# A hybrid attention and convolution backbone on one core: where the second stage's input tiles are split into high and low parts

## The chip, the cores and the metric

The kernel runs on one core of one Trainium2 chip. The metric is device microseconds (us) of one execution. Before the change the median of three runs is 3134.49 us (3130.92, 3134.49 and 3137.77).

## What is computed

Two layers over 2048 latent tokens of width 1024, with a context prefix of 256 tokens. Layer 0 is a multi-head latent attention. Layer 1 is a Conformer convolution module, and the change lies at its start:

```python
def conformer_conv_branch(h, w_in, w_dw, b_dw, g_ln, b_ln, w_o):
    a, bgl, g = jnp.split(h @ w_in, 3, axis=-1)
    u = a * jax.nn.sigmoid(bgl)
    u = lax.conv_general_dilated(u, w_dw, window_strides=(1,), padding=[(CONV_PAD, CONV_PAD)],
                                 dimension_numbers=('NWC', 'WIO', 'NWC'),
                                 feature_group_count=CONV_W) + b_dw
    u = jax.nn.silu(layer_norm(u, g_ln, b_ln)) * jax.nn.silu(g)
    return u @ w_o
```

Here `h` is 2048 x 1024 and `w_in` is 1024 x 3072. Everything is float32. A product is made of three TensorE passes over operands that are each split into a rounded high part and a low remainder (high x high, high x low, low x high: `split3`, L93 to L97).

## The kernel before

The program runs five stages one after the other: `front`, `attention`, `attn_out`, `conv_in`, `conv_out`. The change is in `conv_in` (L1444 to L1868), which makes `h @ w_in`, the gates and the depthwise convolution.

**The input.** `h` comes from `attn_out` through memory as 32 tiles of 128 x 512 (256 KB each; tile n is the slice n % 8 of the width and the block n // 8 of the tokens). Each tile passes three steps. SyncE loads it (`load_h`, L1519) into one of four staging buffers: two are the halves of `ci_gb`, two are made of `ci_raw`. ScalarE copies it to the high part (`h_high`, L1602, tile `h1hi`). VectorE subtracts to get the low part (`h_low`, L1780, tile `h1lo`), which frees the buffer: SyncE waits for `h_low` of tile n - 4 before it loads tile n. The high and low parts of all 32 tiles stay in SBUF for the whole stage.

**The groups.** The width of the output is done in 8 groups of 128 channels. In a group TensorE makes for each block b of 512 tokens a product B (the sigmoid's input, bank 2b) and a product A (bank 2b + 1), of 24 matmuls each, and afterwards four gate products G. From the second group on it also does, after each of the eight A and B products, one chunk of the convolution of the group before. Banks are used in turn, n % 6 for the n-th product of a group: the seventh product (B of block 3, here called B3; the names B0, A0, B1, ... follow) goes into the bank of B0 and waits until ScalarE has made the sigmoid of B0 (`s_sig`); the eighth waits until VectorE has multiplied A0 by that sigmoid (`s_mul`). In the first group each B product also waits, slice by slice, for the `h_low` of its own tiles (`s_hlo`): B0 for tiles 0 to 7, B1 for 8 to 15, B2 for 16 to 23, B3 for 24 to 31.

**The order on the engines.** Every engine has a fixed order of its own. Before the change ScalarE and VectorE go through all 32 tiles first, and only then enter the loop over groups (`loop`, `body`), where the first sigmoid, the copy of the third weight (`w_high` of G) and the first product by a sigmoid (`product`, L1702, which makes `ci_ub`) stand. SyncE likewise loads all 32 tiles, waits for the last `h_low`, and only then starts on the taps, the next group's weights (`load_w`, 512 KB each, L1504) and the stores of `ci_ub` (`store_u`, L1536, 256 KB each, written in pieces of 64 numbers). GpSimd has only the bands of the convolution (L1863).

Of the kernel before, what the change touches and what calls it, by code (L numbers as in the profile page):

```python
# [16 lines left out]

# [1 line left out]

# [1422 lines left out]
def conv_in(nc, net, hhi, hlo, z0, zs, qs):  # L1444
# [9 lines left out]
    with nc.cleanup_on_exit(), ExitStack() as st:  # L1454
# [24 lines left out]
        staged = [t[:, r].rearrange("p s n -> p (s n)") for t in (gb,) for r in range(2)] + [  # L1479
            raw[:, 2 * r:2 * r + 2].rearrange("p s n -> p (s n)") for r in range(2)]  # L1480
        NH = NBLK * KD
        block = st.enter_context(nc.Block())
        B, A, G = range(3)

        def h_tile(t, n):
            return t[:, n % KD, n // KD * BLK:(n // KD + 1) * BLK]
# [29 lines left out]
        @block.sync  # L1516
        def _(sp):
            def load_h(n):
                sp.dma_start(staged[n % 4], net.h1[n % KD, :, n // KD * BLK:(n // KD + 1) * BLK]).then_inc(s_h[n % 4], 16)  # L1519

            load_w(sp, 0, B)
            for n in range(4):
                load_h(n)
            load_w(sp, 0, A)
            sp.dma_start(mask[:], net.mask_in).then_inc(s_const, 16)
            sp.dma_start(bdw[:], net.b_dw).then_inc(s_const, 16)
            for n in range(4, NH):
                sp.wait_ge(s_hlo, n - 3)
                load_h(n)
                if n == KD:  # L1530
                    load_w(sp, 0, G)
            sp.wait_ge(s_hlo, NH)

            def store_u(g, b):
                sp.wait_ge(s_mul, g * 8 + (b + 1))
                sp.dma_start(columns(net.u_phases, g, b), ub[:, b % 2]).then_inc(s_ust[b % 2], 16)  # L1536

            def store_gate(g, b):
                sp.wait_ge(s_mul, g * 8 + (NBLK + b + 1))
                sp.dma_start(columns(net.gate1, g, b), gb[:, b % 2]).then_inc(s_gst[b % 2], 16)  # L1540

            def reload_u(g, q):
                if q + 4 < CH:
                    sp.wait_ge(s_ulo, g * CH + (q + 1))
                    load_u(sp, g, q + 4)

            def store_z(g, q):
                sp.wait_ge(s_z, g * CH + (q + 1))
                sp.dma_start(net.z_chunks[bass.ds(g * CH + q, 1)].rearrange("a p n -> p (a n)"),
                             zb[:, q % 2]).then_inc(s_zst[q % 2], 16)  # L1550

            def body(g, first, last):
                if not first:
                    sp.wait_ge(s_tlo, g)
                sp.dma_start(taps[:], net.taps[bass.ds(g, 1)].rearrange("a p q t -> p (a q) t")).then_inc(s_taps, 16)
                for n in range(CH):
                    if not first:
                        reload_u(g - 1, n)
                        if n:
                            store_z(g - 1, n - 1)  # L1560
                    if not last and n < 3:
                        sp.wait_ge(s_wlo, g * 3 + (n + 1))
                        load_w(sp, g + 1, n)
                    if n % 2:
                        store_u(g, n // 2)
                if not first:
                    store_z(g - 1, CH - 1)
                for k in range(2):
                    sp.wait_ge(s_ust[k], g * 32 + 32)
                for q in range(4):  # L1570
                    load_u(sp, g, q)
                if not last:
                    for b in range(NBLK):
                        store_gate(g, b)
                else:
                    for x in TAIL:
                        if isinstance(x, int):
                            reload_u(g, x)
                            store_z(g, x)
                        else:  # L1580
                            store_gate(g, int(x[1]))

            loop(sp, body)
            for k in range(2):
                sp.wait_ge(s_gst[k], 32 * GROUPS)
                sp.wait_ge(s_zst[k], 64 * GROUPS)
# [12 lines left out]
        def _(act):  # L1599
# [5 lines left out]
            for n in range(4):  # L1605
                h_high(n)
            w_high(act, 0, A, True)
            for n in range(4, NH):
                h_high(n)

            def sigmoid(g, n, src, first):
# [30 lines left out]
            def body(g, first, last):  # L1642
                if first:
                    act.wait_ge(s_const, 32)
                    act.wait_ge(s_pad, 1)
                else:
                    u_high(g - 1, 0)
                for n in range(CH):
                    if not first:
                        if n:  # L1650
                            evict_z(g - 1, n - 1)
                        if n + 1 < CH:
                            u_high(g - 1, n + 1)
                    if n % 2 == 0:
                        act.wait_ge(s_ab, g * 8 + (n + 1))
                        sigmoid(g, n // 2, ps[:, n % 6], first)
                    if n == 0:
                        w_high(act, g, G, first)
                if not first:
                    evict_z(g - 1, CH - 1)  # L1660
                if not last:
                    for s in (B, A):
                        w_high(act, g + 1, s, False)
                act.wait_ge(s_taps, g * 16 + 16)
                if not first:
                    act.wait_ge(s_bhi, g * CH)
                nc.scalar.activation(thi[:], taps[:], ACT.Copy).then_inc(s_thi, 1)
                if not last:
                    for b in range(NBLK):
                        gate(g, b)  # L1670
                else:
                    gate(g, 0)
                    u_high(g, 0)
                    u_high(g, 1)
                    for x in TAIL[1:]:
                        if isinstance(x, int):
                            evict_z(g, x)
                            if x + 2 < CH:
                                u_high(g, x + 2)
                        else:  # L1680
                            gate(g, int(x[1]))
# [5 lines left out]
        def _(dve):  # L1687
# [45 lines left out]
            def gate(g, b):  # L1733
                product(g, NBLK + b, gb[:, b % 2], ps[:, (8 + b) % 6],
                        None if isinstance(g, int) and g == 0 and b < 2 else (s_gst[b % 2], g * 32 + 16 * (b // 2)))

            def body(g, first, last):
                if first:
                    dve.wait_ge(s_const, 32)
                else:  # L1740
                    band_and_low(g - 1, 0)
                for n in range(CH):
                    if not first and n + 1 < CH:
                        band_and_low(g - 1, n + 1)
                    if not first and n:
                        chunk_sums(g - 1, n - 1)
                    b = n // 2
                    if n % 2:
                        dve.wait_ge(s_ab, g * 8 + (n + 1))
                        product(g, b, ub[:, b % 2], ps[:, n % 6],  # L1750
                                None if first and b < 2 else (s_ust[b % 2], g * 32 + 16 * (b // 2)))
                    if n == 1:
                        w_low(g, G)
                if not first:
                    chunk_sums(g - 1, CH - 1)
                if not last:
                    for s in (B, A):
                        w_low(g + 1, s)
                dve.wait_ge(s_thi, g + 1)
                if not first:  # L1760
                    dve.wait_ge(s_blo, g * CH)
                nc.vector.tensor_tensor(tlo[:], taps[:], thi[:].bitcast(F32), ALU.subtract).then_inc(s_tlo, 1)  # L1762
                if not last:
                    for b in range(NBLK):
                        gate(g, b)
                else:
                    gate(g, 0)
                    band_and_low(g, 0)
                    band_and_low(g, 1)
                    for x in TAIL[1:]:  # L1770
                        if isinstance(x, int):
                            if x + 2 < CH:
                                band_and_low(g, x + 2)
                            chunk_sums(g, x)
                        else:
                            gate(g, int(x[1]))

            def h_low(n):
                dve.wait_ge(s_hhi, n + 1)
                nc.vector.tensor_tensor(h_tile(hlo, n), staged[n % 4], h_tile(hhi, n).bitcast(F32),  # L1780
                                        ALU.subtract).then_inc(s_hlo, 1)

            w_low(0, B)
            for n in range(4):
                h_low(n)
            w_low(0, A)
            for n in range(4, NH):
                h_low(n)
            loop(dve, body)
            add_squares(GROUPS * CH - 1)  # L1790
# [470 lines left out]
```

## Time and profile before

| what | value |
|---|---|
| median of three runs | 3134.49 us |
| the profiled execution's own time | 3137.61 us |
| its span, first to last instruction | 3135.7 us |
| TensorE busy | 2933.1 us, 94% |
| VectorE busy | 1817.4 us, 58% |
| ScalarE busy | 1448.3 us, 46% |
| GpSimd busy | 430.2 us, 14% |
| mean granted TensorE clock | 0.983 |

`conv_in` runs from about 2251 us to about 2907 us of the span, and its first group of products from 2258 to 2337 us. Busy shares are averages over the whole span; the change touches some 45 us of it, so that it is read from the timeline of that stretch. In a timeline the columns are start (us from the start of the span), duration (us), engine, line, operation, output and inputs, shape, how many were merged, and in brackets how long the engine sat idle before and what ended that.

### The profile page before, as it was taken

To read this page: it belongs to the slowest core of one execution; us is meant where nothing else is said; L and a number is where in the kernel's file an instruction comes from. 1 tells how busy PE (TensorE), PEld (TensorE's weight loads), DVE (VectorE), ACT (ScalarE), POOL (GpSimd) and SP (SyncE) were. 2 spreads that over 40 slices of the span, in tenths; PEclk is the share of its full clock that TensorE was granted. 3 is DMA by queue.
4 is the path that set the end of the run, shared out by engine and by line. 5 is a ranking of instruction groups with operands and counts; after the bars stand their busy time and mean duration, and the time that the engine had idled before them with its cause. 6 is when DMAs were issued, how large, how long until landed. Compare 5 with 4: busy or idle time off the path is not lost. (4 is left out here: it accounts for less than half of the span.)

```text
span 3135.7 us, 44436 instructions
## 1 busy us (share of the span) xinstructions
PE 2933.1 (94%) x14789; PEld 2436.3 (78%) x14789; DVE 1817.4 (58%) x3135; ACT 1448.3 (46%) x3063; POOL 430.2 (14%) x493
## 2 busy tenths in 40 slices
PE   2999999789999999999999999799799999999698
PEld 2877878578887888878787888678578888888587
DVE  6645545366766776767676676544344444445775
ACT  2544545346555565555555565444432222222553
POOL 1000000012222122222122222100001111112000
PEclk9999999899999999999999999899899999999899
DMA  6556454521211111111212110154442222222563
GB/s 218 173 167 214 165 199 153 192 78 41 70 33 47 56 57 57 51 45 39 72 41 69 34 31 28 69 190 161 147 139 76 76 75 70 73 69 63 180 196 123
DMA packets 225010, 316.59 MB, mean 101 GB/s; under 512 B 81920, under 2 KB 143632, under 8 KB 223632
## 3 DMA queue, kind: packets, MB, share of 16 engines
q1 hardware_dynamic: 220176, 305.37, 30.2%
q10 hardware_dynamic: 4608, 8.39, 0.7%
q8 instruction: 119, 1.95, 0.3%
q14 instruction: 107, 0.88, 0.1%
HBM read 213.95 MB, written 99.75 MB: 100 GB/s over the span
## 5 line engine op out<-in xcount | busy, mean ns | idle before, releaser
L1095 DVE TENSOR_TENSOR at_ptlo<-at_T,at_pthi 128x512 fp32r<-128x512 f32 x576 | 396.8, 689 | 325.0 <-ACT at_pthi L972 321.8
L956 ACT ACTIVATE at_prob<-at_S,at_nmax 128x512 f32<-128x512 f32 (+1 forms) x640 | 411.0, 658 | 371.9 <-DVE at_nmax L1070 360.6
L972 ACT ACTIVATE at_pthi<-at_T 128x512 fp32r<-128x512 f32 x576 | 348.7, 608 | 214.1 <-PE at_T L841 214.1
L1059 DVE TENSOR_REDUCE at_mx<-at_S 128x1 f32<-128x512 f32 (+1 forms) x640 | 393.7, 631 | 75.3 <-PE at_S L816 70.7
L841 PE MATMUL at_T<-ident,at_prob 128*128 128x128 f32 x2304 | 345.7, 272 | 3.2 <-DVE at_ptlo L1095 3.2
L841 PEld LDWEIGHTS at_T<-ident,at_prob 128*128 128x128 f32 x2304 | 279.0, 140 | 68.0 <-DVE at_ptlo L1095 12.5
L95 PE MATMUL ci_ps<-h1hi,ci_whi 128*128 128x512 f32 x768 | 301.8, 393 | 18.0 <-DVE h1lo L1780 12.3
L96 PE MATMUL ci_ps<-h1lo,ci_whi 128*128 128x512 f32 x768 | 300.9, 392 | 0.0
L97 PE MATMUL ci_ps<-h1hi,ci_wlo 128*128 128x512 f32 x768 | 300.6, 391 | 0.0
L811 PE MATMUL at_S<-at_khi,at_qhi 128*128 128x512 f32 (+1 forms) x640 | 249.6, 390 | 46.6 <-ACT at_prob L956 23.8
L95 PE MATMUL at_O<-at_pthi,at_vhi 128*128 128x512 f32 x576 | 270.5, 470 | 3.3 <-issue 2.7
L516 DVE TENSOR_TENSOR fr_wlo<-fr_w,fr_whi 128x1024 fp32r<-128x1024 f32 (+1 forms) x99 | 114.6, 1159 | 251.9 <-ACT fr_whi L388 251.7
L815 PE MATMUL at_S<-at_krhi,at_qr 128*128 128x512 f32 (+1 forms) x640 | 239.0, 373 | 0.0
L813 PE MATMUL at_S<-at_khi,at_qlo 128*128 128x512 f32 (+1 forms) x640 | 238.4, 372 | 0.0
L816 PE MATMUL at_S<-at_krlo,at_qr 128*128 128x512 f32 (+1 forms) x640 | 237.8, 372 | 0.0
L812 PE MATMUL at_S<-at_klo,at_qhi 128*128 128x512 f32 (+1 forms) x640 | 237.5, 371 | 0.0
L97 PE MATMUL at_O<-at_pthi,at_vlo 128*128 128x512 f32 x576 | 227.5, 395 | 0.0
L96 PE MATMUL at_O<-at_ptlo,at_vhi 128*128 128x512 f32 x576 | 227.5, 395 | 0.0
L1863 POOL TENSOR_TENSOR ci_blo<-ci_tlo,ci_mask 128x640 fp32r<-128x640 f32 x64 | 108.4, 1701 | 787.2 <-DVE ci_tlo L1762 433.1
L1210 POOL TENSOR_TENSOR at_dgx<-ident,at_rl 128x128 f32<-128x128 f32 x128 | 51.1, 400 | 1079.0 <-DVE at_dghi L1087 1079.0
L95 PE MATMUL fr_ps<-fr_hhi,fr_whi 128*128 128x512 f32 (+1 forms) x472 | 185.3, 393 | 4.9 <-DVE fr_rob L571 1.8
L811 PEld LDWEIGHTS at_S<-at_khi,at_qhi 128*128 128x128 f32 x640 | 120.8, 189 | 83.8 <-ACT at_prob L956 33.2
(221 smaller groups left out, 6116.0 us busy)
## 6 DMA issues: line engine op xcount, KB each, us to landing
fr_w<-in_w_front SPq DMA_DIRECT2D x75, 512.0 KB, 4.1
at_wmod<-in_w_mod SPq DMA_DIRECT2D x32, 512.0 KB, 3.4
ci_w<-in_cv_w_in SPq DMA_DIRECT2D x24, 512.0 KB, 4.1
fr_w<-in_w_front SPq DMA_DIRECT2D x24, 384.0 KB, 4.0
values<-fr_ob SPq DMA_DIRECT2D x36, 256.0 KB, 2.8
at_kst<-k_nope SPq DMA_DIRECT2D x8, 1152.0 KB, 7.6
at_vst<-values SPq DMA_DIRECT2D x8, 1152.0 KB, 8.2
fr_x<-in_x SPq DMA_DIRECT2D x16, 512.0 KB, 6.7
```

The costliest lines, as they stand in the source:

```text
L95: nc.tensor.matmul(out, whi, xhi, start=first, stop=False)
L96: nc.tensor.matmul(out, whi, xlo, start=False, stop=False)
L97: return nc.tensor.matmul(out, wlo, xhi, start=False, stop=last)
L811: nc.tensor.matmul(out, qhi[:, r, q], khi[:, k], start=True, stop=False)
L813: nc.tensor.matmul(out, qlo[:, r, q], khi[:, k], start=False, stop=False)
L815: nc.tensor.matmul(out, qr[:, r, q], krhi[:, k], start=False, stop=False)
L816: nc.tensor.matmul(out, qr[:, r, q], krlo[:, k], start=False, stop=True).then_inc(s_qk, 1)
L841: mm = nc.tensor.transpose(out[:, i * P:(i + 1) * P], prob[:, j % 2, i, kt * P:(kt + 1) * P], net.ident[:])
L956: nc.scalar.activation(prob[:, j % 2, i, k], S[:, c, 0:k.stop - k.start], ACT.Exp, scale=SCALE, bias=nmax[:, i % 2:i % 2 + 1], accum_out=l ...
L972: nc.scalar.activation(dst, T[:, (n + SLOTS * j) % 2], ACT.Copy).then_inc(s_hi, 1)
L1059: nc.vector.tensor_reduce(mx[:, i % 2, c:c + 1], S[:, c, 0:k.stop - k.start], AXX, ALU.max).then_inc(s_mx, 1)
L1095: nc.vector.tensor_tensor(ptlo[:, kt % 3], T[:, (n + SLOTS * j) % 2], pthi[:, kt % 3].bitcast(F32), ALU.subtract).then_inc(s_lo, 1)
```

## The change

In the first group the 32 tiles are no longer all split ahead of the loop. Tiles 0 to 7 are split ahead of it as before. Tiles 8 to 31 are split inside the first body, between its steps n = 0 to 7:

- n = 0: ScalarE does `h_high` of 8 to 11, the first sigmoid, `h_high` of 12 to 15, the weight copy `w_high` of G; VectorE does `h_low` of 8 to 15.
- n = 1: tiles 16 to 19; then VectorE does the first product (`ci_ub`) and `w_low` of G.
- n = 2: tiles 20 to 23, then on ScalarE the second sigmoid.
- n = 3: tiles 24 to 27; then VectorE does the second product.
- n = 4: tiles 28 to 31, then on ScalarE the third sigmoid.

SyncE loads tiles up to 11 ahead of the body, then G's weight (before, that stood behind tile 8) and the taps. Inside the body it loads 12 to 15 and the next group's weight B, 16 to 19 and weight A and `store_u` of block 0, 20 to 23 and weight G, 24 to 27 and `store_u` of block 1, 28 to 31. The wait for the last `h_low` moves behind the stores. TensorE's program and GpSimd's are the same.

```diff
+        def split_behind(n):
+
+            m = KD + 4 * (n + 1)
+            return (range(KD, KD + 4), range(KD + 4, m + 4)) if n == 0 else (range(m, min(m + 4, NH)), range(0))
+
...
-            for n in range(4, NH):
+            def reload_h(n):
                 sp.wait_ge(s_hlo, n - 3)
                 load_h(n)
-                if n == KD:
-                    load_w(sp, 0, G)
-            sp.wait_ge(s_hlo, NH)
+
+            for n in range(4, KD + 4):
+                reload_h(n)
+            load_w(sp, 0, G)
...
                 for n in range(CH):
-                    if not first:
+                    if first:
+                        for x in range(KD + 4 * (n + 1), min(KD + 4 * (n + 2), NH)):
+                            reload_h(x)
+                    else:
                         reload_u(g - 1, n)
                         if n:
                             store_z(g - 1, n - 1)
...
                 for k in range(2):
                     sp.wait_ge(s_ust[k], g * 32 + 32)
+                if first:
+                    sp.wait_ge(s_hlo, NH)
                 for q in range(4):
                     load_u(sp, g, q)
...
             w_high(act, 0, A, True)
-            for n in range(4, NH):
+            for n in range(4, KD):
                 h_high(n)
...
                 for n in range(CH):
-                    if not first:
+                    if first:
+                        for x in split_behind(n)[0]:
+                            h_high(x)
+                    else:
                         if n:
                             evict_z(g - 1, n - 1)
                         if n + 1 < CH:
...
                         act.wait_ge(s_ab, g * 8 + (n + 1))
                         sigmoid(g, n // 2, ps[:, n % 6], first)
+                    if first:
+                        for x in split_behind(n)[1]:
+                            h_high(x)
                     if n == 0:
                         w_high(act, g, G, first)
...
                     if not first and n:
                         chunk_sums(g - 1, n - 1)
+                    if first:
+                        for x in itertools.chain(*split_behind(n)):
+                            h_low(x)
                     b = n // 2
...
             w_low(0, A)
-            for n in range(4, NH):
+            for n in range(4, KD):
                 h_low(n)
             loop(dve, body)
```

## Rows read from the trace of the kernel before

**Rows 1.** The page's first part: busy time, share, instructions of each engine.
```profile
PE 2933.1 (94%) x14789; PEld 2436.3 (78%) x14789; DVE 1817.4 (58%) x3135; ACT 1448.3 (46%) x3063; POOL 430.2 (14%) x493
```
**Rows 2.** Waits of TensorE, 2250 to 2345 us: total us, times, longest us.
```profile
PE ci_ps L95 <- DVE h1lo L1780: 12.3, 2, 10.9
PE ci_ps L95 <- ACT ci_sig L1615: 5.7, 1, 5.7
```
**Rows 3.** Waits of TensorE, 2345 to 2920 us, those in this stage.
```profile
PE ci_ps L95 <- DVE ci_ulo L1730: 0.6, 1, 0.6
```
**Rows 4.** Timeline of TensorE around its wait, start, us, operation.
```profile
2295.12 0.39 PE L97 MATMUL ci_ps<-h1hi,ci_wlo 128*128 128x512 f32 x1
2301.19 0.80 PE L95 MATMUL ci_ps<-h1hi,ci_whi 128*128 128x512 f32 x1 [5.69 <-ACT ci_sig L1615]
...
2306.48 0.41 PE L95 MATMUL ci_ps<-h1hi,ci_whi 128*128 128x512 f32 x1
```
**Rows 5.** Windows: stretch and its us, busy (count) by engine, PEclk, DMA share, GB/s.
```profile
2301.00:2306.00 5.00, 4.81 (x11) 3.82 (x12) 3.09 (x3) 2.06 (x4) 0.00 (x0) 0.50 1.05 316
```
**Rows 6.** Timeline of ScalarE around the first sigmoid.
```profile
2299.25 1.28 ACT L1615 ACT_TABLE_LOAD   x1
2300.54 0.60 ACT L1615 ACTIVATE ci_sig<-ci_ps 128x512 f32<-128x512 f32 x1
2301.04 1.05 ACT L1596 ACTIVATE ci_whi<-ci_w 128x1024 fp32r<-128x1024 f32 x1
...
2309.44 0.60 ACT L1615 ACTIVATE ci_sig<-ci_ps 128x512 f32<-128x512 f32 x1 [6.38 <-PE ci_ps L97]
```
**Rows 7.** Timeline of VectorE: tiles 18 and 19, tile 31, first and last product.
```profile
2281.68 1.36 DVE L1780 TENSOR_TENSOR h1lo<-ci_raw,h1hi 128x512 fp32r<-128x512 f32 x2 [0.19 <-ACT h1hi L1602]
...
2299.27 0.69 DVE L1780 TENSOR_TENSOR h1lo<-ci_raw,h1hi 128x512 fp32r<-128x512 f32 x1 [1.69 <-ACT h1hi L1602]
2301.28 1.08 DVE L1702 TENSOR_TENSOR ci_ub<-ci_ps,ci_sig 128x512 f32<-128x512 f32 x1 [1.32 <-ACT ci_sig L1615]
...
2314.88 1.11 DVE L1702 TENSOR_TENSOR ci_ub<-ci_ps,ci_sig 128x512 f32<-128x512 f32 x1 [6.95 <-PE ci_ps L97]
```
**Rows 8.** Timeline of all engines, loads of tiles 8, 9 and 12 and splits.
```profile
2264.45 0.32 SPq L1519 DMA_DIRECT2D ci_gb<-h  x1
...
2265.29 0.43 SPq L1519 DMA_DIRECT2D ci_gb<-h  x1
...
2268.27 0.63 ACT L1602 ACTIVATE h1hi<-ci_gb 128x512 fp32r<-128x512 f32 x1 [2.57 <-DMA ci_gb<-h]
...
2269.66 2.24 SPq L1519 DMA_DIRECT2D ci_gb<-h  x2
2270.19 0.63 ACT L1602 ACTIVATE h1hi<-ci_gb 128x512 fp32r<-128x512 f32 x1 [1.28 <-DMA ci_gb<-h]
```
**Rows 9.** Landing of the tile loads of all 32 tiles, 2250 to 2345 us.
```profile
DMA to landing us min/median/max: 3.0/4.1/6.0
```
**Rows 10.** DMA issues with KB each and median us to landing, 2262 to 2273 us.
```profile
ci_raw<-h SPq DMA_DIRECT2D x4, 256.0 KB, 4.4
```
**Rows 11.** The same, 2273 to 2300 us.
```profile
ci_gb<-h SPq DMA_DIRECT2D x8, 256.0 KB, 3.6
```
**Rows 12.** The same, 2250 to 2345 us, the stores of the first group.
```profile
u_phases<-ci_ub SPq DMA_DIRECT2D x4, 256.0 KB, 3.6
```
**Rows 13.** Timeline of TensorE in the attention: two other waits and what followed.
```profile
638.05 0.50 PE L811 MATMUL at_S<-at_khi,at_qhi 128*128 128x512 f32 x1 [1.72 <-ACT at_prob L956]
...
654.16 0.55 PE L811 MATMUL at_S<-at_khi,at_qhi 128*128 128x512 f32 x1 [3.55 <-ACT at_prob L956]
...
657.91 0.40 PE L816 MATMUL at_S<-at_krlo,at_qr 128*128 128x512 f32 x1
```
**Rows 14.** Windows, the stretches behind these two waits.
```profile
638.00:642.00 4.00, 3.94 (x17) 3.30 (x18) 1.60 (x3) 2.46 (x9) 0.00 (x0) 1.00 0.00 0
...
654.10:658.00 3.90, 3.84 (x10) 3.06 (x11) 0.69 (x1) 2.47 (x9) 0.71 (x2) 0.56 0.01 4
```

More of the change, by code:

```diff
@@ L20 @@
+import itertools
 from contextlib import ExitStack
@@ L1735, in gate, with h_low @@
                         None if isinstance(g, int) and g == 0 and b < 2 else (s_gst[b % 2], g * 32 + 16 * (b // 2)))
+            def h_low(n):
+                dve.wait_ge(s_hhi, n + 1)
+                nc.vector.tensor_tensor(h_tile(hlo, n), staged[n % 4], h_tile(hhi, n).bitcast(F32),
+                                        ALU.subtract).then_inc(s_hlo, 1)
             def body(g, first, last):
@@ L1776, in body @@
                             gate(g, int(x[1]))
[L1778 to L1781, printed above, removed]
             w_low(0, B)
```

## The prediction, made before the changed kernel was run

> **What bounds the kernel now.** I read the page's busy shares first: TensorE is busy 94% of the span [rows 1], so the time can only fall where TensorE stands still or runs at its lower clock. Next come the waits of TensorE in the stretch that the change touches [rows 2]. There are three. Two are on `h_low`, 12.3 us together, 10.9 of them the start of the stage, where the first weight and tile have to arrive; the change leaves everything up to tile 7 alone, so these stay. The third is 5.7 us and ends with the first sigmoid. The timeline shows it between A2's last matmul and B3's first [rows 4]. ScalarE shows the reason: its table load for the sigmoid begins at 2299.25 us, straight behind the last tile, and the sigmoid at 2300.54 [rows 6], although its input was ready since B0. B3 then pays a second time. Its first 12 matmuls take 2306.48 - 2301.19 = 5.29 us [rows 4], with a granted clock of 0.50, the 1.2 GHz level, after 5.69 us of standing still [rows 5]. At full clock a product of 24 matmuls lasts 5.44 us, the distance from B3's sigmoid at 2309.44 [rows 6] to A3's product at 2314.88 [rows 7], or 0.227 us a matmul; 12 are 2.72 us, so the clock costs 2.57 us.
>
> So the prize has a fixed size. A2 ended at 2295.5 us (2295.12 + 0.39), B3 at 2309.44: 13.9 us for work of 5.44, a loss of 8.5 us. After A3's end at 2314.88 TensorE has almost no wait left in the stage: two of 0.6 us, of which one stands in [rows 3]. Whatever moves A3's end therefore moves the end of the kernel by the same amount, and the sum is one number: A3's end in the new order.
>
> **What the change adds.** The work stays the same: no instruction more or fewer on any engine. What costs is the new place of `store_u` in SyncE's queue. Block 0's store now stands between the loads of tiles 19 and 20. It waits for VectorE's first product, and VectorE does that product behind `h_low` of tile 19. So tile 20 is not requested when its buffer comes free (at `h_low` of 16), but only after all four buffers have been emptied. The stream of tiles runs dry once there, and once more at block 1's store, between tiles 27 and 28. Before, the stream was already only just ahead of TensorE: the last `h_low` starts at 2299.27 us [rows 7], 3.8 us after A2's end.
>
> **Durations.** From landing to the reuse of its buffer a tile needs 1.4 us (ScalarE takes tile 8 at 2268.27, its buffer is loaded again at 2269.66 [rows 8]). A load lands 3.0 to 6.0 us after issue, median 4.1 [rows 9]; 4.4 behind others and a weight [rows 10]; 3.6 in the even stretch [rows 11]. Issues that stand in a row follow at about 0.45 us (three from 2264.45 to 2265.29, the middle one being G's weight [rows 8]). A product by a sigmoid takes 1.08 us [rows 7].
>
> **Step by step.**
> 1. Tiles 8 to 19. `h_low` of 19 ended at 2283.04 us (2281.68 + 1.36 [rows 7]). For the change: tile 9 landed 1.92 us after tile 8 though issued 0.84 after it, with G's weight between them [rows 8]; that weight now goes behind tile 11, which gives up to 1.1 us. Against it: G's weight and the taps now lie ahead of tile 12 and the next group's B ahead of tile 16, each worth up to the same 1.1 us; and the table load and sigmoid, 1.28 + 0.60 us [rows 6], come between tiles 11 and 12 on ScalarE, where it mostly waits for tile 12 anyway. The weight copy behind the first sigmoid came without another table load [rows 6], so going back and forth between copies and sigmoids costs one load, as before. I take 2283.0, with bounds of 2282.5 and 2284.0. B1 and A1 are then done about when they were.
> 2. First product and store: 2284.1; tiles 20 to 23 are issued from 2284.6 to 2286.0. With 4.1 us for the first and 4.4 for the last, `h_low` of 20 ends at 2284.6 + 4.1 + 1.4 = 2290.1 and of 23 at 2291.8. B2 ends three matmuls later, 2292.5, and A2 at 2297.9, 2.4 us later than before. The next group's weight A and G, which go out around here, are why I don't take 3.6.
> 3. Tiles 24 to 27 are issued as 20 to 23 are split: `h_low` of 27 ends at 2291.8 + 4.1 + 1.4 = 2297.3. B3 starts at once at 2297.9 and runs its first four slices to 2300.6.
> 4. Second product to 2298.4, store, tiles 28 to 31 issued from 2298.9 to 2300.3. `h_low` of 28 ends at 2298.9 + 5.5 = 2304.4, of 31 at 2300.3 + 5.8 = 2306.1. TensorE stands still from 2300.6 to 2304.4, 3.8 us.
> 5. The clock. No row has this gap. The nearest is one of 3.55 us, after which the granted clock was 0.56 for 3.9 us (in the main 1.2 GHz) and 9 matmuls took 657.91 - 654.16 = 3.75 us instead of 2.04, 1.7 us lost; after 1.72 us it stayed at 1.00, 2.4 GHz [rows 13, 14]. I take 1.7, with bounds of 0 and 2.57. B3 ends at 2304.4 + 2.72 + 1.7 = 2308.8, A3 at 2314.3.
>
> Sum: 2314.3 - 2314.88 = -0.6 us. The 8.5 us of before come back as 2.4 in B2, 3.8 in front of B3's fifth slice and 1.7 of clock, 7.9 together. The rest is covered: the third sigmoid, of B2, comes behind tile 31 on ScalarE and frees the bank of the third gate product, 10 us later; the convolution of group 0 starts only in group 1, and `ci_ub` of block 3 is stored as soon after A3 as before.
>
> **A rule weighed.** The stores go out in pieces of 64 numbers, and one leads each burst. Their landing took 3.6 us, no longer than the 4.1 of a tile load of the same 256 KB [rows 9, 12]. The Trainium skill (DMA: Bandwidth & Descriptors, Specifications) states that transfers below 512 B miss line rate, because they are done as read-modify-write; that speaks against having them ahead of loads that TensorE waits for. If a store took the queues for the time of one more tile, by the page an estimate of about 0.7 us a burst, the result would be nearly 1 us worse than my sum. By the trace's landing times it is nothing.
>
> **Rivals.**
> - *The stream refills fast.* The loads land in 3.0 us, the shortest of rows 9, and the last of a burst in 3.6. Then `h_low` of 19 ends at 2282.5, of 20 at 2288.5, of 23 at 2290.4; A2 ends at 2296.5 and B3's fourth slice at 2299.2. `h_low` of 27 ends at 2294.8, of 28 at 2300.8 and of 31 at 2302.7: a gap of 1.6 us, with no loss of clock by the 1.72 us row. A3 ends at 2308.9, 6.0 us sooner: 3128.5. For it: 3.6 us was the median in the even stretch. Against: these bursts have a store and weights beside them.
> - *Slower: the queue behind the store.* Each burst of a store, four tiles and a weight fills the queues, and its tiles land in the 6.0 us that the slowest took [rows 9], in the middle round in 4.4. From 2284.0: `h_low` of 23 at 2294.3, A2 ends at 2300.4, B3's fourth slice at 2303.1, `h_low` of 27 at 2300.1, the product at 2301.2, tile 28 issued at 2301.65 and split by 2309.05. The gap is 6 us with the clock loss of 2.57: B3 ends at 2314.4, A3 at 2319.8, 4.9 us later: 3139.4. Its point of decision is the end of B3: later than 2309.44 loses. For it: the burst at 2262 to 2273 us, with one weight in it, had a median of 4.4 [rows 10]. Against: only single tiles took 6.0.
> - *Nothing runs dry.* If the loads kept their old pace in spite of the stores, B3 would follow A2 without a gap and 8.5 us would go: 3126. SyncE's order excludes that, as I read it; I leave 3 in 100 for having read it wrongly.
>
> **How the numbers follow.** The sum stands against the profiled execution: 3137.61 - 0.6 = 3137.0 us. That execution lies 3.1 us above the median of the three runs, whose spread (3130.92 to 3137.77) includes it; against the median it is 3134.49 - 0.6 = 3133.9, which I give. A measurement of this kernel tells about 0.2%, 6.3 us, from no change. Chances: the forecast, within some 3 us, 0.50; fast refill 0.25; slower queue 0.22; no drying 0.03. Faster by over 6.3 us needs the third or the better end of the first: 0.12. Slower by over 6.3 us needs the second with more loss still: 0.11. The same: 0.77. The range goes from the first rival's 3128.5 to the second's 3139.4, with some 1.6 us of run spread on each side: 3127 to 3141.
>
> **What would show it.** TensorE's wait on the first sigmoid is gone; in its place stand waits on `h_low`, in B2 around tile 20 (2 to 3 us) and in B3 at tile 28 (3 to 4 us). SyncE waits for `ci_ub`'s product between tiles 19 and 20 and between 27 and 28, and no load is on its way during either. A granted clock near 0.5 shows in B3's second half. I am wrong if A3 ends more than 3 us from 2314.3 with the start of the stage as before, if TensorE doesn't wait at tile 28, or if a stretch outside the first group moves.

## The result and the profile after

The changed kernel takes 3143.16 us (median of 11 runs, 3138.83 to 3150.67) against 3137.42 us for the kernel before, timed beside it on the same chips. The ratio is 1.0021 with a 95% interval of 1.0014 to 1.0029: 6.6 us slower, between 4.4 and 9.1. The prediction had 3133.9 us, with a range of 3127 to 3141 and 0.11 on slower. The profiled execution of the changed kernel took 3141.1 us, its span is 3139.1 us.

Busy time shows nothing, as was to be expected when no work is added. The page's first part, to be set beside [rows 1]:

```profile
PE 2934.4 (93%) x14789; PEld 2437.4 (78%) x14789; DVE 1817.1 (58%) x3135; ACT 1448.5 (46%) x3063; POOL 430.1 (14%) x493
```

The waits of TensorE between 2250 and 2345 us (engine, line, for whom: total us, times, longest), the answer to [rows 2]:

```profile
PE ci_ps L96 <- DVE h1lo L1758: 18.5, 5, 10.8
```

The wait on the first sigmoid is gone, all of it, and everything is now a wait on `h_low`. Those of SyncE in the same stretch name the cause:

```profile
SPq L1544 <- DVE ci_ub L1721: 25.4, 4, 7.0
SPq L1526 <- DVE h1lo L1758: 19.6, 20, 3.7
```

L1544 is `store_u`. SyncE stands 25.4 us at the four stores (12.2 us before), and tile loads are queued behind two of them. The timeline of SyncE, ScalarE, VectorE and TensorE at the first of these (start, us, engine, operation, in brackets the idle time before and what ended it):

```profile
2284.42 0.69 DVE L1758 TENSOR_TENSOR h1lo<-ci_raw,h1hi 128x512 fp32r<-128x512 f32 x1 [1.71 <-ACT h1hi L1615]
2285.03 1.07 DVE L1721 TENSOR_TENSOR ci_ub<-ci_ps,ci_sig 128x512 f32<-128x512 f32 x1
...
2286.13 0.67 SPq L1544 DMA_DIRECT2D u_phases<-ci_ub  x1
...
2286.84 1.24 SPq L1526 DMA_DIRECT2D ci_gb<-h  x2
...
2288.13 0.91 SPq L1526 DMA_DIRECT2D ci_raw<-h  x2
...
2289.09 0.43 SPq L1511 DMA_DIRECT2D ci_w<-in_cv_w_in  x1
...
2291.83 1.28 ACT L1615 ACTIVATE h1hi<-ci_gb 128x512 fp32r<-128x512 f32 x2 [7.43 <-DMA ci_gb<-h]
...
2293.23 0.79 PE L96 MATMUL ci_ps<-h1hi,ci_whi 128*128 128x512 f32 x1 [4.97 <-DVE h1lo L1758]
```

One reads it downward as a chain: `h_low` of tile 19, the product behind it, the store, and only then the loads of tiles 20 to 23, although the buffer of tile 20 had been free for over 4 us (`h_low` of 16 and 17 end by 2282.1). No tile is on its way from 2283.8 to 2286.8. ScalarE gets tile 20 at 2291.83, 4.99 us after issue, and TensorE has stood still for 4.97 us in the middle of B2. The second place, tiles 28 to 31:

```profile
2300.51 1.08 DVE L1721 TENSOR_TENSOR ci_ub<-ci_ps,ci_sig 128x512 f32<-128x512 f32 x1
2301.61 0.58 SPq L1544 DMA_DIRECT2D u_phases<-ci_ub  x1
2302.24 1.25 SPq L1526 DMA_DIRECT2D ci_gb<-h  x2
...
2307.05 1.32 ACT L1615 ACTIVATE h1hi<-ci_gb 128x512 fp32r<-128x512 f32 x2 [7.18 <-DMA ci_gb<-h]
...
2308.46 0.50 PE L96 MATMUL ci_ps<-h1hi,ci_whi 128*128 128x512 f32 x1 [1.85 <-DVE h1lo L1758]
```

A3's product, the answer to the last of [rows 7], and the windows (busy us and count for PE, PEld, DVE, ACT and POOL, granted clock, DMA share, GB/s) behind B2's wait:

```profile
2316.99 1.11 DVE L1721 TENSOR_TENSOR ci_ub<-ci_ps,ci_sig 128x512 f32<-128x512 f32 x1 [5.60 <-PE ci_ps L98]
```
```profile
2293.20:2300.00 6.80, 6.77 (x20) 5.41 (x21) 4.07 (x7) 4.20 (x7) 0.00 (x0) 0.65 0.61 211
```

The clock fell to the 1.2 GHz level behind B2's wait, not behind B3's. The stage began 1.45 us later than in the profile before, an offset from stages that the change doesn't touch (over the fourteen profiles of this study, all with the same program up to here, the stage's first matmul lies between 2255.5 and 2266.9 us). So I measure from the first matmul of the stage to A3's end, here called **the group**: 56.5 us before, 57.2 us after in these two profiles. Behind A3 the stage takes the same in both: its last product with the input starts 591.3 us later.

A difference of 0.7 us in the one pair of profiles, 6.6 us in the times: either the group varies, or the cause lies elsewhere. That was the first thing to settle.

### The profile page after: what moved, and what is told of

It reads as the page before. It is cut to its first block and busy times, and to the rows that moved or that the text cites. A ratio compares the mean times of both kernels' runs of the same rounds, so it can differ in the third digit from the quotient of the medians.

```text
span 3139.1 us, 44437 instructions
## 1 busy us (share of the span) xinstructions
PE 2934.4 (93%) x14789; PEld 2437.4 (78%) x14789; DVE 1817.1 (58%) x3135; ACT 1448.5 (46%) x3063; POOL 430.1 (14%) x493
```

## Experiments

Theories: **queue**, the stores' waits on VectorE's products hold up the tile loads behind them on SyncE; **traffic**, the store and the next group's weights delay the tiles that are loaded beside them; **elsewhere**, something outside the first group. All ratios are to the kernel before on the same chip. The same view of each gives the table at the end of this section.

**The same kernels again.** The changed kernel (`again`, `again_2`) and the one before (`before_again`, `before_again_2`), unedited.

> The changed kernel once more, nothing edited, to see how much of its 0.21% belongs to the first group. One profile of each kernel gave 57.15 us from the first matmul of the stage to A3's end after the change and 56.49 before, only 0.66 us more, while the medians lie 5.7 us apart. If the first group is the whole cause, its length here must come out several us above 57.15 in at least some executions, with a longer loss of clock behind a gap. If it stays within 1 us of 57.15, the rest of the 0.21% arises elsewhere in the program, in stages that the change does not touch, and the ratio to the kernel before should still be 1.001 to 1.003.

> The changed kernel a third time, one look, for the spread of its first group: 57.2 and 63.4 us from the first matmul to A3's end in the two profiles so far, the longer one with the lower clock behind both gaps. Either value can come; a value near 57 again would make the long one the exception, one in between or above would show that the loads' landing and the clock's fall behind the second gap vary from execution to execution.

> The kernel before, unedited, for the spread of its own first group: one profile gave 56.5 us from the first matmul to A3's end. The changed kernel's three gave 57.2, 63.4 and 61.1, mean 60.6, 4.1 us more, where the medians ask for 6.6 us with an interval of 4.4 to 9.4. If the first group explains the whole, this one should lie at or somewhat below 56.5, because B3 waits here for the last tile and the sigmoid, and tiles that come sooner shorten it. If it comes out at 59 or more, the first group explains less than half and something outside remains.

> The same once more. Together with the two other profiles of the kernel before it gives a mean and a spread of the first group. Theory: 53 to 57 us, with the wait for the first sigmoid between 3 and 6 us long and the lower clock behind it. Rival: as wide a spread as the changed kernel's, 6 us, in which case three profiles of each can't carry the comparison.

`again` has a ratio of 1.0021 (1.0012 to 1.0030), as the first time. The groups of the changed kernel are 57.2, 63.3 and 61.1 us, mean 60.5; those of the kernel before 56.5, 55.7 and 52.0, mean 54.7. The 5.8 us between the means lie within the 4.4 to 9.1 of the times. Elsewhere is not needed to explain the difference, but it isn't measured as nothing either: behind A3 this stage takes 591.3 to 591.4 us to its last product with the input in all fourteen profiles (in `sigmoid_alone` from A3's end as taken below), and from there to the last instruction it is 229.5, 229.5 and 230.5 us before and 230.8, 231.3 and 230.8 after, where the other kernels spread over 229.5 to 231.5. Three profiles of each are few. The first pair had met the changed kernel's best group, and the executions of `again` and `again_2` (3149.1 and 3152.12 us) were slower than the changed kernel's median. Its worst, `again`, in windows behind the two waits:

```profile
2296.00:2302.00 6.00, 5.29 (x13) 4.13 (x14) 3.48 (x6) 3.57 (x6) 0.00 (x0) 0.50 0.81 276
2312.50:2319.50 7.00, 6.38 (x16) 4.98 (x17) 3.52 (x5) 2.89 (x5) 0.00 (x0) 0.52 0.18 50
```

Here the clock was lost twice. In `again_2` it fell behind the first wait, and for 3.4 us shortly after the second. The kernel before varies as well: in `before_again_2` the wait for the sigmoid was 3.51 us and no clock was lost, so that its group of 52.0 us lies below the expected 53 to 57, without the expected lower clock.

**Stores behind the tiles** (`store_late`). On SyncE only:

```diff
-                    if n % 2:
+                    if n % 2 and not (first and n < 4):
                         store_u(g, n // 2)
+                    if first and n in (2, 4):
+                        store_u(g, n // 2 - 1)
```

> Only SyncE's order differs from the changed kernel: the stores of blocks 0 and 1 stand behind the loads of tiles 20 to 23 and 28 to 31, so no tile load waits for a product. Theory of the queue (the store's wait dries the stream): both long waits of TensorE on h_low (4.97 and 1.85 us) shrink to under 1 us, the tile stream runs evenly and A3 ends about 7 us sooner after the stage's first matmul, near 50 us; ratio to before about 0.998. Theory of contention (weights and stores beside the tiles are what delays them): the weights and stores still go out in the same stretch, so waits of 2 to 4 us remain and the ratio stays at 1.000 to 1.002.

The ratio is 0.9990 (0.9981 to 0.9999), group 50.6 us, and no wait of TensorE inside the products of blocks 1 to 3 is longer than 0.89 us. Two DMAs of 256 KB moved behind four others turn 6.6 us of loss into about 3 us of gain. The expected group (near 50) was met, the expected ratio (0.998) not quite; the range that contention would have given, 1.000 to 1.002, was missed too.

**The wait without the store in front** (`wait_only`). As `store_late`, but SyncE keeps the wait:

```diff
                     if first:
+                        if n in (2, 4):
+                            sp.wait_ge(s_mul, n // 2)
                         for x in range(KD + 4 * (n + 1), min(KD + 4 * (n + 2), NH)):
                             reload_h(x)
```

> The changed kernel with the same waits of SyncE for the products of blocks 0 and 1 ahead of tiles 20 and 28, but the two stores themselves issued behind the four tile loads. It tells the wait from the store's traffic. In the changed kernel the first tile of each burst landed 5.0 and 4.8 us after issue, where 4.1 was expected. If the small pieces of the store in front hold the tiles up, they now land near 4 us and TensorE's waits get about 1 us shorter each. If four tiles issued together simply land together late, they stay at 4.8 to 5.0 us and the time is that of the changed kernel.

Ratio 1.0005 (0.9995 to 1.0014), group 56.5 us. It differs from `store_late` by the wait alone: the wait takes back the 3.1 us which that kernel gains and ends no better than the kernel before, and the rest of the loss needs the store in front. Its timeline at the first burst:

```profile
2286.69 1.08 DVE L1725 TENSOR_TENSOR ci_ub<-ci_ps,ci_sig 128x512 f32<-128x512 f32 x1
...
2287.80 0.80 SPq L1526 DMA_DIRECT2D ci_gb<-h  x2
...
2291.14 1.38 ACT L1619 ACTIVATE h1hi<-ci_gb 128x512 fp32r<-128x512 f32 x2 [5.09 <-DMA ci_gb<-h]
```

Tile 20 lands 3.34 us after issue instead of 4.99, and is issued 0.03 us behind the product instead of 0.74: 2.4 us sooner in all, where the expectation had it land near 4 us. TensorE's wait there is 2.27 us, and 1.64 at tile 28. The last tile of the burst gains less: tile 23 lands 4.67 us after issue instead of 5.19, and counted from the product's end 6.0 us instead of 7.7.

**The early sigmoid alone** (`sigmoid_alone`), an edit of the kernel before: ScalarE makes the first sigmoid behind tile 11, and nothing else moves.

```diff
             for n in range(4, NH):
                 h_high(n)
+                if n == KD + 3:
+                    act.wait_ge(s_ab, 1)
+                    sigmoid(0, 0, ps[:, 0], True)
...
-                    if n % 2 == 0:
+                    if n % 2 == 0 and not (first and n == 0):
```

> The kernel before with one step moved: ScalarE makes the first sigmoid behind tile 11 instead of behind tile 31. VectorE's and SyncE's orders are those of before. If the first sigmoid is the whole of the wait of 5.69 us, B3 starts at once behind A2 and is paced by tiles 24 to 31, whose last one is split 4.5 us after A2's end; the first product by a sigmoid, still behind tile 31 on VectorE, then frees A0's bank about 1 us late for A3. A3's end comes 7 to 8 us sooner, near 49 us after the first matmul, and the ratio is 0.9975. If the new place of the table load and the sigmoid holds the tiles up by more than a microsecond, B1 waits for its tiles longer than before and the gain is under 5 us.

Ratio 0.9978 (0.9969 to 0.9987), the fastest of all: 3131.22 us, 6.9 us below the kernel before by the ratio. The group is 47.2 us (A3's end taken from ScalarE's next weight copy at 2307.91, which waits for it; the product by the sigmoid came later here, behind the store of block 1). Between B1 and A3 TensorE has no wait left that the profile lists. ScalarE around the moved sigmoid:

```profile
2273.94 1.28 ACT L1613 ACT_TABLE_LOAD   x1
2275.23 0.60 ACT L1613 ACTIVATE ci_sig<-ci_ps 128x512 f32<-128x512 f32 x1
2275.73 0.62 ACT L1602 ACTIVATE h1hi<-ci_gb 128x512 fp32r<-128x512 f32 x1
```

Table load and sigmoid fall mostly into the time in which ScalarE would have waited for tile 12: `h_low` of 12 ends 16.4 us after the first matmul, where it was 15.9 in the kernel before, and no product waits for it. The expected 7 to 8 us are met against the mean group of before (54.7 - 47.2 = 7.5); the profile from which they were reckoned, at 56.5, would give 9.3, and the end near 49 us that the expectation named was beaten by nearly 2.

**The next group's weights behind tile 31** (`weights_late`), and the same with both waits but no traffic beside the bursts (`bare_wait`), and with neither (`both_late`). The common edit:

```diff
-                    if not last and n < 3:
+                    if not last and n < 3 and not first:
                         sp.wait_ge(s_wlo, g * 3 + (n + 1))
                         load_w(sp, g + 1, n)
+                    if first and n == 4:
+                        for s in range(3):
+                            sp.wait_ge(s_wlo, s + 1)
+                            load_w(sp, 1, s)
```

> The changed kernel with the next group's three weights (512 KB each) loaded behind tile 31 instead of between the tiles; the stores and their waits stay ahead of tiles 20 and 28. If weights beside the tiles are part of the loss, h_low of tile 19 ends about 1 us sooner after the stage's first matmul than in the changed kernel (25.2 and 27.5 us in its two profiles), tiles 24 to 27 follow each other more closely, and the ratio drops from 1.0021 to about 1.0010. If only the stores' place matters, the ratio stays at 1.002. Were the weights the main cause, it would fall to 0.998.

> Only the waits are left: SyncE still waits for the products of blocks 0 and 1 ahead of tiles 20 and 28, but the stores go behind the four tiles and the next group's weights behind tile 31, so that nothing shares the two bursts. The wait alone then costs what lies between this and the kernel with the early sigmoid alone (0.9978). Theory: each burst lands 3.3 to 3.9 us after issue, gaps of 1 to 2.5 us remain, the clock does not fall; ratio 0.999 to 1.000. If the traffic was everything and the wait nothing, 0.998.

> Stores of blocks 0 and 1 behind the next four tiles without a wait ahead of them, and the weights behind tile 31. ScalarE and VectorE keep the changed kernel's order. If the place of the stores and of the weights is all that the changed kernel loses, this one must reach the kernel with the early sigmoid alone: 0.9978, A3's end near 48.5 us after the first matmul. If it stays at 0.999, the products between the tiles on VectorE, or the weight copy on ScalarE, cost something too.

`weights_late`: 1.0013 (1.0004 to 1.0022). `bare_wait`: 1.0002 (0.9993 to 1.0011). `both_late`: 0.9984 (0.9975 to 0.9993), TensorE's waits inside blocks 1 to 3 are 0.18 and 0.22 us. These four kernels differ by one step each and add up the loss: from `both_late` to `bare_wait` the wait, +0.0018 (5.6 us); to `weights_late` the store in front, +0.0011 (3.5 us); to the changed kernel the weights, +0.0008 (2.5 us). Each step is a difference of two ratios with 0.0009 on either side, so it is uncertain by up to 0.0013: by the ratios the wait's step is clear and the other two are not. The store's step is borne out on the same chip by the medians, 3137.92 us in `bare_wait` and 3141.22 in `weights_late`, and by the lengths of the bursts in the table below.

The weights' step stands on its ratio, which overlaps, on the two other pairs that differ by it (`store_late` to `both_late` 0.0006, `wait_only` to `bare_wait` 0.0003), and on the place of tile 19: its `h_low` ends 25.3, 27.5 and 26.9 us after the first matmul in the changed kernel, 26.9 in `store_late`, 27.0 in `wait_only` and 25.9 and 28.1 in the last two kernels below, all with the weights, and 25.6, 25.2 and 24.6 without (24.7, 24.4 and 24.6 in the kernel before). The means are 1.7 us apart. From `h_low` of 11 to that of 19, the stretch in which the next group's B goes out, it is 10.7 to 13.1 us in the seven with it and 9.5 to 10.4 in the three without. So the sign of the weights' step is shown and its size only roughly.

Of what had been expected, `weights_late` met its ratio (about 1.0010, though its interval just includes the rival's 1.002 too) and its tile 19, but tiles 24 to 27 came no closer together (6.8 us from `h_low` of 23 to that of 27, against 5.4, 6.9 and 6.3), and its wait at tile 28, 5.30 us, was longer than any that the changed kernel showed. `bare_wait` met the waits of 1 to 2.5 us (1.30 and 1.24) without a fall of the clock and came just above its ratio of 0.999 to 1.000. `both_late` met the group (48.5), and its interval includes the 0.9978 that was expected.

**Is it the store, or its small pieces?** (`front_small`, `front_wide`). As `wait_only`, with an extra store of 256 KB ahead of each burst, into memory that is overwritten later; the two kernels differ in how it is laid out. The cuts show the store alone.

```diff
                             sp.wait_ge(s_mul, n // 2)
+                            b = n // 2 - 1
+                            sp.dma_start(columns(net.z_phases, GROUPS - 1, b), ub[:, b]).then_inc(s_dec[b], 16)
```

and for `front_wide`

```diff
                             sp.wait_ge(s_mul, n // 2)
+                            b = n // 2 - 1
+                            sp.dma_start(net.z_phases[GROUPS - 1, :, 2 * b:2 * b + 2, :].rearrange("p s n -> p (s n)"), ub[:, b].rearrange("p s n -> p (s n)")).then_inc(s_dec[b], 16)
```

> SyncE waits for the products of blocks 0 and 1 ahead of tiles 20 and 28; behind each wait, ahead of the four tiles, goes an extra store of the same 256 KB in pieces of 64 numbers into memory that is overwritten much later, and the real store behind the four tiles. With the store behind, the first tile of the first burst landed 3.3 us after issue, with it in front 5.0. This one must show about 5.0 again if the store in front is what delays the tiles, and the ratio should be near the changed kernel's 1.002.

> As the last one, but the extra store in front goes out in pieces of 512 numbers, 8 times as long, for the same 256 KB. If the small pieces are what holds the tiles up, the first tile of each burst lands 3.3 to 4.0 us after issue instead of 5.0, and the group is 2 to 3 us shorter than with small pieces in front. If any store of 256 KB in front does it, it is 5.0 as well and the two kernels take the same time.

The timeline of `front_small` and then of `front_wide` at the first burst:

```profile
2288.18 0.67 SPq L1570 DMA_DIRECT2D z_phases<-ci_ub  x1
2288.89 1.24 SPq L1527 DMA_DIRECT2D ci_gb<-h  x2
...
2293.76 1.26 ACT L1624 ACTIVATE h1hi<-ci_gb 128x512 fp32r<-128x512 f32 x2 [7.33 <-DMA ci_gb<-h]
...
2295.07 0.63 ACT L1624 ACTIVATE h1hi<-ci_raw 128x512 fp32r<-128x512 f32 x1
...
2296.18 0.63 ACT L1624 ACTIVATE h1hi<-ci_raw 128x512 fp32r<-128x512 f32 x1 [0.48 <-DMA ci_raw<-h]
```
```profile
2288.44 0.34 SPq L1570 DMA_DIRECT2D z_phases<-ci_ub  x1
2288.82 0.93 SPq L1527 DMA_DIRECT2D ci_gb<-h  x2
...
2292.22 0.63 ACT L1624 ACTIVATE h1hi<-ci_gb 128x512 fp32r<-128x512 f32 x1 [5.54 <-DMA ci_gb<-h]
...
2295.03 0.63 ACT L1624 ACTIVATE h1hi<-ci_gb 128x512 fp32r<-128x512 f32 x1 [2.17 <-DMA ci_gb<-h]
...
2295.71 1.29 ACT L1624 ACTIVATE h1hi<-ci_raw 128x512 fp32r<-128x512 f32 x2
```

With small pieces in front the first tile lands 4.87 us after issue (5.28 in the second burst), with wide ones 3.40 (3.39): for the first tile the small pieces do it, and they take SyncE 0.67 us to issue instead of 0.34. The other three tiles tell otherwise. Behind the wide store they land 5.71, 5.89 and 6.08 us after issue, behind the small one 4.78, 4.87 and 5.50, and counted from the end of the product tile 23 lands 7.9 and 8.0 us later: the burst as a whole is as long with either. From `h_low` of 19 to that of 23 it is 10.4 us with small pieces and 10.3 with wide ones (second burst 10.2 and 10.1), against 8.4 (8.2) in `wait_only`, with no store in front. So an extra store of 256 KB in front costs a burst about 2 us however it is laid out; why the wide one holds up the later tiles instead of the first wasn't tried.

The times agree with that: `front_small` has 1.0028 (1.0017 to 1.0039), `front_wide` 1.0021 (1.0012 to 1.0030). The one group of the latter is 61.7 us, longer than the other's 60.3: its tile 19 came 2.2 us later, ahead of the bursts, and B1 already waited 2.25 us there. The landing of the first tile was foretold rightly, the shorter group not, and nothing here shows that wide pieces save time.

| kernel | ratio to before | group, us | first tile of the two bursts, us from issue | `h_low` of 19 to 23; of 27 to 31, us |
|---|---|---|---|---|
| before | 1 | 56.5, 55.7, 52.0 | no burst | 6.0, 6.1, 5.0; 4.4, 4.6, 4.8 |
| changed | 1.0021 | 57.2, 63.3, 61.1 | 4.99, 4.93, 5.04; 4.81, 4.57, 4.54 | 10.1, 10.0, 10.2; 9.8, 9.6, 9.5 |
| front_small | 1.0028 | 60.3 | 4.87; 5.28 | 10.4; 10.2 |
| front_wide | 1.0021 | 61.7 | 3.40; 3.39 | 10.3; 10.1 |
| weights_late | 1.0013 | 60.9 | 4.41; 4.77 | 9.5; 10.6 |
| wait_only | 1.0005 | 56.5 | 3.34; 3.16 | 8.4; 8.2 |
| bare_wait | 1.0002 | 53.2 | 3.13; 3.14 | 8.4; 8.2 |
| store_late | 0.9990 | 50.6 | no burst | 4.5; 4.8 |
| both_late | 0.9984 | 48.5 | no burst | 5.1; 6.0 |
| sigmoid_alone | 0.9978 | 47.2 | no burst | 5.1; 4.8 |

The groups and the ratios go together: from `sigmoid_alone` to the changed kernel it is 13.3 us by the groups and 13.5 by the ratios. The first group therefore carries the loss, with the reservation of one profile for most kernels.

## Why the prediction was wrong

The chain of waits held. TensorE's wait on the sigmoid went away, SyncE's stores took its place where the text said, and the two waits came at tiles 20 and 28. What failed are two terms of the sum: step 1 let the weights cancel, and steps 2 and 4 priced the bursts as if no store stood in front of them. Both waits were mis-sized with that, 4.7 to 5.0 us in B2 for a forecast of 2.4 and 1.9 to 3.3 at tile 28 for 3.8. What happened is the rival "the queue behind the store": slower by 6.6 us where it was priced at 4.9 and given 0.22. Its total is near, its own terms are not all: it had the tiles land in 6.0 us (4.9 to 5.0 measured), a gap of 6 us at tile 28, and tile 19 at 25.6 us, 1 us early. Counted from the stage's first matmul (2258.39 before), the forecast had `h_low` of 31 at 47.7 us; the three profiles have 50.6, 54.0 and 52.9, mean 52.5, so 4.8 us late. A3's end was forecast at 55.9 and came at 60.5 on average, 4.6 us late. The whole error is in the stream of tiles:

- **Step 1, tiles 8 to 19: 2.0 us too small.** Forecast 24.6, mean 26.6. I let the weight taken away (G, ahead of tile 9) and the weights put in (G and taps ahead of 12, next B ahead of 16) cancel. They don't: with the next group's weights behind tile 31 it is 25.6, 25.2 and 24.6.
- **Step 2, the first burst: 1.3 us too small.** From `h_low` of 19 to that of 23 it is 10.1, 10.0 and 10.2 us, forecast 8.8. The first tile's landing was taken as 4.1 us, the median of all tile loads, and measured 4.93 to 5.04; the last one's as 4.4, and measured 5.1 to 5.4. The rest is the issuing: tile 23 was forecast 1.9 us behind the product's end and went out 2.5 us behind it.
- **Step 3, tiles 24 to 27: 0.7 us too small**, 5.4, 6.9 and 6.3 us from `h_low` of 23 to that of 27, forecast 5.5. This round varies most.
- **Step 4, the second burst: 0.8 us too small**, from 27 to 31 9.8, 9.6 and 9.5 us against 8.8.
- **Step 5, the clock: right in sum by luck, wrong in place.** From `h_low` of 31 to A3's end it is 6.6, 9.4 and 8.2 us, mean 8.1, forecast 8.2. I took 1.7 us once, in B3. The waits in B2 were 4.97, 4.68 and 4.80 us, and the lower clock followed each: in the first profile B2's next 11 matmuls take 2298.02 - 2293.23 = 4.79 us instead of 2.50, a loss of 2.3. That loss lay mostly in time that B3 would have waited for tile 28 anyway, so it shortened B3's waits to 1.85, 2.69 and 3.26 us (forecast 3.8). `again` paid the whole a second time, `again_2` a part.

The first profile alone would have hidden most of this. Its A3 ends 57.2 us after the first matmul, 1.2 us from the forecast and within the 3 us that the text had set as its sign of being wrong. That was luck: its step 1 was the shortest of the three, and it lost no clock in B3. In `again` A3's end is 7.4 us off.

**The rule weighed.** The text set a rule of the Trainium skill (DMA: Bandwidth & Descriptors, Specifications: transfers below 512 B miss line rate, since they are done as read-modify-write) against the landing of the stores themselves, 3.6 us [rows 12], and gave it nothing. That row answers another question: how long a store takes, not how long the loads queued behind it are held. On the rule itself this case agrees in direction: the extra store of 256 KB lands 3.3 and 3.2 us after issue in pieces of 64 numbers and 2.6 and 2.7 in pieces of 512 (us to landing in the last column, first burst, `front_small` and then `front_wide`):

```profile
z_phases<-ci_ub SPq DMA_DIRECT2D x1, 256.0 KB, 3.3
```
```profile
z_phases<-ci_ub SPq DMA_DIRECT2D x1, 256.0 KB, 2.6
```

But the loss of a burst isn't explained by it, since the burst is as long behind the wide store. What the text put at nothing is the store in front itself: 1.4 to 1.9 us a burst between `wait_only` and the changed kernel, about twice the estimate of 0.7.

**The range and the chances.** The range was built from the landing times of rows where no store stood ahead of the loads. Its upper end, 3141, took the slowest landing, 1 us more for step 1, the larger loss of clock and 1.6 us of run spread; step 1 came out 2 us late, since the weights had been taken as balanced within 1 us. And it was set around the median of the first three runs, 3134.49 us; eleven runs of the same kernel have 3137.42. The profile that the sum stood on, at 56.5 us, also had the longest group of the three of its kernel, 1.8 us above their mean. So the 9.3 us between the forecast and the measured median come out as 4.6 from the chain above, 1.8 from that profile and 2.9 from the reference; the first two are means of three profiles that spread over 6.1 and 4.5 us, so that the sum fits to the tenth by luck.

The stage stays bound by what the forecast said: the second rival's point of decision, B3's end later than before, is crossed in all three profiles, by 0.7, 6.5 and 4.6 us against the profile that it was read from.

## What to carry to other kernels

Before an item is moved ahead on an issuing queue, write down what it waits for and what is queued behind it: a store that waits for a product holds up every load behind it until the buffers are empty, and then the refill costs a full landing time each time round, and some 1.5 to 2 us more when the store itself goes out ahead of the loads. If one step is late, move that step alone: the early sigmoid by itself gains 6.9 us, while the change that also carried the stores and weights along loses 6.6. And one profile of each kernel is not enough to balance a sum of a few microseconds: the same group of the same kernel took from 57.2 to 63.3 us.

## What the runs showed of the hardware

- A store of 256 KB ahead of four tile loads on the same queue makes the burst about 2 us longer (10.4 and 10.3 us against 8.4, `front_small`, `front_wide` and `wait_only`). In pieces of 64 numbers it delays all four landings, the first by 1.5 to 1.9 us against the same store in pieces of 512 numbers; in pieces of 512 it leaves the first alone and delays the other three more (5.5 to 6.1 us after issue). The small pieces take 0.67 us instead of 0.34 to issue. The tile load issued right behind it took 0.66 us to issue in the changed kernel, where 0.32 is usual.
- The length of a wait alone doesn't decide on the clock. After 2.69 us of wait in `again` the granted clock was 0.52 over the next 7 us, the 1.2 GHz level; after 2.27 us in `wait_only` and 3.26 us in `again_2` it fell 1.1 to 1.6 us behind the restart. After 3.32 us in `weights_late` and 3.51 us in `before_again_2` it stayed at 1.00 for the next 3 us, the 2.4 GHz level. In all of these the profile lists no gap in TensorE for some microseconds ahead of the wait. What else decides wasn't tried. The forecast, which took the loss from the row of nearest length, read more out of that row than it holds. The windows behind the waits in `weights_late`, `before_again_2`, `again_2` and `wait_only`, in this order (the granted clock is the third number from the end):

```profile
2290.90:2294.00 3.10, 3.09 (x13) 2.49 (x14) 1.94 (x3) 1.69 (x3) 0.00 (x0) 1.00 0.53 152
```
```profile
2299.60:2303.00 3.40, 3.40 (x15) 2.81 (x16) 3.15 (x3) 1.90 (x3) 0.00 (x0) 1.00 0.97 313
```
```profile
2317.90:2321.00 3.10, 3.10 (x9) 2.40 (x10) 2.88 (x4) 1.66 (x3) 0.00 (x0) 0.65 0.00 1
```
```profile
2292.50:2297.50 5.00, 4.95 (x14) 3.53 (x15) 2.13 (x4) 2.40 (x5) 0.00 (x0) 0.67 1.00 344
```

- Stages in front of the change move by up to 11 us between executions whose program is the same up to there (first matmul at 2255.5 to 2266.9 us; 2259.8 to 2266.9 in the three of the changed kernel), so that a stage has to be measured from its own start.
